# Gated products split tile by tile out of PSUM, a new branch order in the merge, and state-space constants in two parts

## The chip, the cores and the metric

The kernel runs on one core of a Trainium2 chip. Its time is the device time of one execution in microseconds. TensorE multiplies matrices into PSUM, VectorE and ScalarE can read and write PSUM and SBUF, GpSimd works on SBUF alone, and SyncE issues the DMAs that bring weights from HBM. Each engine has its own instruction stream, and they wait for one another through semaphores that are written out by hand in the code.

## What is computed

One decoder layer over two groups of tokens, 256 of a prompt and 64 of a sample, which lie side by side as 320 columns (N). D_MODEL is 2048 and D_FF 5632; everything is float32.

```
x += 0.5 * (silu(h @ w_gate) * (h @ w_up)) @ w_down          # h = RMSNorm(x), first block
z  = RMSNorm(x) @ w_in          # u_ssm, c_q, c_kv, k_r, q_mem, three gates
y_ssm = GLU(gelu(S5(u_ssm)))    # state space: 64 groups of 64 complex modes
y_mla = latent attention(c_q, c_kv, k_r)                     # 16 heads
y_mem = attention to 256 memory tokens(q_mem)                # 4 heads
x += (sig(g_ssm)*(y_ssm@W_ssm) + sig(g_mla)*(y_mla@W_mla) + sig(g_mem)*(y_mem@W_mem)) @ w_out
x += 0.5 * (silu(h @ w_gate) * (h @ w_up)) @ w_down          # second block
y  = RMSNorm(x)
```

## The kernel before

Activations lie feature-major: a tile is 128 features by 320 token columns. A product in float32 is made of three matmuls in the rounded type `fp32r`: operands are split into a high part (rounded) and a low part (the rest), and `three` (lines 396 to 400) adds hi*hi, hi*lo and lo*hi in one PSUM bank.

Weights come in chunks. A full chunk is 256 rows by 512 columns: SyncE loads it into one of three `raw` slots (`load`), ScalarE rounds it to `whi` (line 388), GpSimd subtracts to get `wlo` (line 393), and TensorE multiplies it in `products`: two row tiles q by four column tiles m, three matmuls each, 24 in all. There are four `whi`/`wlo` slots, so weights can be ready up to four chunks ahead. The counter `w_used` tells that TensorE is done with a chunk. The eight PSUM banks make two halves, 0 and 1, of four banks, one bank per column tile; `half_free` tells that a half was read out.

A feed-forward block is a stream of windows of 512 features. The head is `gate` (8 chunks, half 0) and `up` (8 chunks, half 1). Then a loop of ten runs `gate` of the next window, `down` of this one (8 chunks in four windows w of two, on the halves 1, 0, 1, 0) and `up` of the next one. The tail is the last `down`, on the halves 0, 1, 0, 1. VectorE scales the gate by the norm's `rstd` into `silu_g` when the gate is complete, ScalarE applies SiLU, and after the last `up` chunk VectorE multiplies (`prod`, line 1562), rounds (`phi`, line 1573) and subtracts (`plo`, line 1575); `down` needs `phi` and `plo`. In the head and the loop a whole `gate` window stands between these and their `down`; ahead of the tail's `down` nothing does.

The norm's sum of squares is a matmul with ones into bank 7 (`sums`, line 1055), in the head at the seventh `gate` chunk. VectorE makes the mean (line 1372) and its reciprocal (1375), ScalarE the root (734). `up` uses bank 7, so it waits for the mean.

State-space constants (`s5_constants`) are a chain of over a hundred tiny VectorE operations, each waiting for the one before. They stand in VectorE's stream behind the first block's first `silu_g` scaling, ahead of its first products.

The mixer's input projection runs seven windows (`Z_WIN`). In the first, `sums` stands at the sixth chunk. VectorE then runs `powers(0)`, `powers(1)` and `phases(0)` of the state space, and behind them `mean_inv`; then it copies windows 0 and 1 into `u4` (lines 1718, 1719). The first state-space transposes (line 1135) wait for window 1's copy.

The merge loops over four windows of D_MODEL. For each branch: `gate` (8 chunks, half 0) and `branch` (half 1), whose product with the sigmoid gate VectorE adds into `merged`. The order is state space (4 chunks), attention (8 chunks), memory (4 chunks of half size, 12 matmuls each). After the third, `merged` is split into `mhi` (line 1953) and `mlo` (1954) for `out` (8 chunks), which runs after the next window's first gate, or in the tail at once. The merge loop is at line 527, the feed-forward loop at 487.

Of the kernel before, what the change touches and what calls it, by code (L numbers as in the profile page):

```python
# [17 lines left out]
F32 = mybir.dt.float32  # L18
# [56 lines left out]

GR_MEM = (0, 0)
# [41 lines left out]
def build(nc, t_in, t_out):  # L118
    with ExitStack() as ctx:
# [88 lines left out]
        prod = B.take("prod", [4, N])  # L208
# [105 lines left out]
        prod_set = sem("prod_set")  # L314
        prod_hi = sem("prod_hi")
# [86 lines left out]
        def products(e, c, half, n, width, tiles, ahi, alo, k, first, last, cols=N, i=None, per=0):  # L402
# [5 lines left out]
            for q in range(n):  # L408
                for m in range(tiles):
                    a, b = wh[:, q, m * P:(m + 1) * P], wl[:, q, m * P:(m + 1) * P]  # L410
                    ins = three(e, banks[:, 4 * half + m, 0:cols], a, b, ahi[:, k + q, 0:cols], alo[:, k + q, 0:cols],
                                first and q == 0, last and q == n - 1)
            ins.then_inc(w_used, 1)
# [162 lines left out]
        with nc.Block() as block:  # L576

            @block.sync
            def _(e):
# [96 lines left out]
                def merge_load(c, item, i, step, g):  # L676
# [5 lines left out]
                    elif kind == "gate":  # L682
                        c_at = e.snap(i * WIN + (COL_GATE + b * D + WIN)) if step == "body" else COL_GATE + b * D
# [18 lines left out]
            def _(e):  # L702
# [66 lines left out]
                def ffn(name, c0, gr, g):  # L769
                    if name == "ffn2":  # L770
                        next_h(name, g, c0, gr, 1)
# [6 lines left out]
                    def visit(c, kind, k, b, i, per, step):  # L778
                        if c >= c0 + (4 if name == "ffn1" else 3):
# [9 lines left out]
                        if step == "head" and kind == "up" and k == 2:  # L789
                            root(name, rstd)  # L790
# [258 lines left out]
            def _(e):  # L1049
# [34 lines left out]
                def ffn(name, c0, gr):  # L1084
# [3 lines left out]
                    def visit(c, kind, k, b, i, per, step):  # L1088
                        if kind in ("gate", "up"):
                            half = 0 if kind == "gate" else 1  # L1090
                            if step == "head" and kind == "gate":
                                if k == 6:
                                    if name == "ffn2":
                                        e.wait_ge(half_free[1], gr[1])
                                    sums(name, 7)
                                e.wait_ge(hf_lo, AP[name] + k + 1)
                            if step == "head" and kind == "up" and k == 0:
                                e.wait_ge(half_free[1], gr[1])
                                e.wait_ge(mean_ready, 2 * NORM[name] + 1)
                            if k == 0 and step == "body":  # L1100
                                wait(e, half_free[half], gr[half] + (1 if kind == "gate" else 3), i, 3)
                            products(e, c, half, 2, WIN, 4, hhi, hlo, 2 * k, k == 0, k == 7, N, i, per)
                        else:
                            w = k // 2
                            half = (1, 0, 1, 0)[w] if step == "body" else (0, 1, 0, 1)[w]
                            if k < 2:

                                if step == "body":
                                    wait(e, prod_lo, 2 * sbase + k + 1, i, 2)
                                else:  # L1110
                                    e.wait_ge(prod_lo, 2 * (sbase + FFN_BLOCKS - 1) + k + 1)
# [5 lines left out]
                            products(e, c, half, 2, WIN, 4, phi, plo, 2 * (k % 2), k % 2 == 0, k % 2 == 1, N, i, per)  # L1117
# [57 lines left out]
                for w, (c_at, width, half) in enumerate(Z_WIN):  # L1175
                    for k in range(8):
                        for part, s in s5_at.get(8 * w + k, []):
                            s5_pe(part, s)
                        if k == 0:
                            e.wait_ge(half_free[half], seen[half])  # L1180
                            seen[half] += 1
                        if w == 1 and k == 0:
                            e.wait_ge(mean_ready, 2 * NORM["mix"] + 1)
                        if w == 0:
                            if k == 5:
                                e.wait_ge(half_free[1], GR_Z[1])
                                sums("mix", 7)
                            e.wait_ge(hf_lo, AP["mix"] + k + 1)
                        products(e, CH_Z + 8 * w + k, half, 2, width, width // P, hhi, hlo, 2 * k, k == 0, k == 7)
# [869 lines left out]
```

## Time and profile before

| | us |
|---|---|
| median of 3 runs (3240.90 to 3247.93) | 3242.78 |
| the profiled execution's own time | 3241.28 |
| its span, from the first to the last instruction | 3239.5 |
| TensorE's matmuls busy | 3085.8 |
| VectorE busy | 1190.1 |
| ScalarE busy | 1088.1 |
| GpSimd busy | 2037.8 |

The mean granted TensorE clock is 0.975 of full speed. Times in rows are microseconds from the start of the span unless marked ns. PE is TensorE's matmul stream and PEld its weight loads; DVE is VectorE, ACT ScalarE, POOL GpSimd. A line number is that of the kernel before.

### The profile page before, as it was taken

The page shows a single profiled execution, that of the slowest core. Times are in us where ns is not written, and L with a number is a line of the kernel's source. Part 1 is how long each engine was busy: PE and PEld are TensorE (multiplying, and loading weights), DVE is VectorE, ACT ScalarE, POOL GpSimd, SP SyncE. Part 2 cuts the span into 40 slices and gives each one's busy share as a digit, 9 for nine tenths or more (in the row PEclk, how much of TensorE's full clock was granted, in tenths as well). Part 3 has the DMA queues.
Part 4 walks back from the last instruction along what each step waited for, and adds up shares of the span by engine and source line. Part 5 has one row for each costly group of instructions (what it writes and reads, how often), then busy time and mean ns, then how long its engine had stood idle before and what let it go on. Part 6 is the DMA issues. An engine that isn't in the chain of part 4 may idle for free.

```text
span 3239.5 us, 51544 instructions
## 1 busy us (share of the span) xinstructions
PE 3085.8 (95%) x20534; PEld 3050.3 (94%) x20534; DVE 1190.1 (37%) x1944; ACT 1088.1 (34%) x1369; POOL 2037.8 (63%) x876
## 2 busy tenths in 40 slices
PE   7999999999999889699999999998999999999997
PEld 7999999999999889688899999998999999999996
DVE  8832222222226698756623121212522222222223
ACT  5323333333334344323433333332433333333332
POOL 7656666666666344444476766666666666666663
PEclk9999999999999889899999999999999999999998
DMA  6544544444445232223244544444444444444542
GB/s 216 165 124 149 149 149 149 149 149 149 149 149 156 77 103 68 70 70 96 85 150 144 156 142 147 149 146 132 145 150 149 150 148 150 149 149 149 149 149 98
DMA packets 237692, 442.86 MB, mean 137 GB/s; under 512 B 14161, under 2 KB 33169, under 8 KB 237585
## 3 DMA queue, kind: packets, MB, share of 16 engines
q1 hardware_dynamic: 237584, 441.34, 44.9%
q8 instruction: 78, 1.28, 0.2%
q14 instruction: 30, 0.24, 0.0%
HBM read 436.81 MB, written 4.47 MB: 136 GB/s over the span
## 4 chain that ended last, share of the span: by engine, by line
PE 75%; DVE 11%; POOL 7%; issue 6%; ACT 1%; DMA 0%; POOLq 0%; SPq 0%; DVEq 0%; ACTq 0%
PE banks L398 24%; PE banks L399 23%; PE banks L400 23%; POOL wlo L393 7%; DVE hlo L1394 2%; PE banks L1200 1%; DVE hf L1407 1%; DVE elh L1415 1%; DVE s5v L1415 0%; PE banks L1224 0%; DVE mla_p L1745 0%; PE banks L1166 0%; DVE xs L1671 0%; PE banks L453 0%; PE banks L455 0%
## 5 line engine op out<-in xcount | busy, mean ns | idle before, releaser
L393 POOL TENSOR_TENSOR wlo<-raw,whi 128x1024 fp32r<-128x1024 f32 (+4 forms) x848 | 2006.1, 2369 | 1140.1 <-ACT whi L388 1139.8
L388 ACT ACTIVATE whi<-raw 128x1024 fp32r<-128x1024 f32 (+4 forms) x848 | 868.5, 1027 | 1850.3 <-PE banks L400 1728.7
L398 PE MATMUL banks<-hhi,whi 128*128 128x320 f32 (+1 forms) x4016 | 1253.8, 312 | 51.5 <-issue 14.0
L399 PE MATMUL banks<-hlo,whi 128*128 128x320 f32 (+1 forms) x4016 | 1248.3, 311 | 0.0
L400 PE MATMUL banks<-hhi,wlo 128*128 128x320 f32 (+1 forms) x4016 | 1248.2, 311 | 0.0
L398 PEld LDWEIGHTS banks<-hhi,whi 128*128 128x128 f32 x4016 | 763.9, 190 | 54.9 <-issue 33.5
L399 PEld LDWEIGHTS banks<-hlo,whi 128*128 128x128 f32 x4016 | 763.6, 190 | 0.4 <-issue 0.2
L400 PEld LDWEIGHTS banks<-hhi,wlo 128*128 128x128 f32 x4016 | 762.7, 190 | 0.0
L398 PE MATMUL banks<-phi,whi 128*128 128x320 f32 x1408 | 437.8, 311 | 19.9 <-DVE plo L1575 19.9
L399 PE MATMUL banks<-plo,whi 128*128 128x320 f32 x1408 | 437.4, 311 | 0.0
L400 PE MATMUL banks<-phi,wlo 128*128 128x320 f32 x1408 | 437.3, 311 | 0.0
L1533 DVE SCALAR_TENSOR_TENSOR x<-banks,x 128x320 f32<-128x320 f32 x416 | 175.2, 484 | 542.0 <-PE banks L400 542.0
L398 PEld LDWEIGHTS banks<-phi,whi 128*128 128x128 f32 x1408 | 266.5, 189 | 20.7 <-issue 10.5
L399 PEld LDWEIGHTS banks<-plo,whi 128*128 128x128 f32 x1408 | 266.5, 189 | 0.0
L400 PEld LDWEIGHTS banks<-phi,wlo 128*128 128x128 f32 x1408 | 266.4, 189 | 0.0
L1562 DVE TENSOR_TENSOR prod<-banks,silu_g 128x320 f32<-128x320 f32 x88 | 37.0, 483 | 481.3 <-PE banks L400 481.2
L1551 DVE TENSOR_TENSOR silu_g<-banks,rstd 128x320 f32<-128x320 f32 x88 | 37.0, 484 | 388.4 <-PE banks L400 388.4
L1929 DVE TENSOR_TENSOR gate<-banks,rstd_mix 128x320 f32<-128x320 f32 x48 | 20.2, 484 | 254.6 <-PE banks L400 254.6
L398 PE MATMUL banks<-mhi,whi 128*128 128x320 f32 x256 | 80.1, 313 | 9.6 <-DVE mlo L1954 9.6
L1573 DVE CAST phi<-prod 128x640 fp32r<-128x640 f32 x44 | 81.9, 1861 | 0.0
L399 PE MATMUL banks<-mlo,whi 128*128 128x320 f32 x256 | 79.9, 312 | 0.0
L400 PE MATMUL banks<-mhi,wlo 128*128 128x320 f32 x256 | 79.9, 312 | 0.0
(280 smaller groups left out, 2918.3 us busy)
## 6 DMA issues: line engine op xcount, KB each, us to landing
raw<-i_ffn_w_gate SPq DMA_DIRECT2D x176, 512.0 KB, 3.6
raw<-i_ffn_w_up SPq DMA_DIRECT2D x176, 512.0 KB, 3.7
raw<-i_ffn_w_down SPq DMA_DIRECT2D x176, 512.0 KB, 3.6
raw<-i_w_in SPq DMA_DIRECT2D x136, 512.0 KB, 3.7
raw<-i_w_post SPq DMA_DIRECT2D x80, 512.0 KB, 3.6
raw<-i_w_uq SPq DMA_DIRECT2D x16, 384.0 KB, 3.3
raw<-i_w_mem_k SPq DMA_DIRECT2D x8, 512.0 KB, 4.3
raw<-i_w_mem_v SPq DMA_DIRECT2D x8, 512.0 KB, 4.0
```

Source lines behind the costliest of these rows:

```text
L388: e.activation(whi[:, c % SPL, 0:size], raw[:, slot, 0:size], ACT.Copy).then_inc(w_hi, 1)
L393: e.tensor_tensor(wlo[:, c % SPL, 0:size], raw[:, c % RAW, 0:size], whi[:, c % SPL, 0:size].bitcast(F32), ALU.subtract).then_inc(w_lo, 1)
L398: e.matmul(out, hi_s, hi_m, start=start, stop=False)
L399: e.matmul(out, hi_s, lo_m, start=False, stop=False)
L400: return e.matmul(out, lo_s, hi_m, start=False, stop=stop)
L1200: ins = e.matmul(banks[:, bank, col:col + nk], a, b, start=n_ == 0, stop=n_ == len(ops) - 1)
L1394: ins = e.scalar_tensor_tensor(out=hlo[:, t, 0:cols], in0=src[:, t, 0:cols], scalar=gains[:, g + t:g + t + 1], in1=hhi[:, t, 0:cols].bitca ...
L1407: e.tensor_tensor(a, a, square_at(name, p), ALU.add).then_inc(sq_added, 1)
L1533: ins = e.scalar_tensor_tensor(out=x[:, 4 * w + m], in0=banks[:, 4 * half + m, 0:N], scalar=scale, in1=x[:, 4 * w + m], op0=ALU.mult, op1= ...
L1551: ins = e.tensor_tensor(silu_g[:, m], banks[:, m, 0:N], rstd[:], ALU.mult)
L1562: ins = e.tensor_tensor(prod[:, m], banks[:, 4 + m, 0:N], silu_g[:, m], ALU.mult)
L1573: e.tensor_copy(phi[:, t], prod[:, t]).then_inc(prod_hi, 1)
```

## The change

1. In both feed-forward blocks the last `up` chunk runs column tile by column tile, and each of its first three tiles signals `tile_done`. VectorE multiplies each tile in place in PSUM, copies it to `phi` and subtracts to `plo`; `prod` is gone. `down` waits per tile.
2. The same for the third branch of the merge, whose sum with `merged` is also made in PSUM. The branch order becomes state space, memory, attention.
3. In the merge's tail `out` uses the halves 0, 1, 0, 1 and not 1, 0, 1, 0; the second block starts accordingly.
4. `sums` stands ahead of the first `up` chunk (in the mixer, ahead of the second window). That chunk does its first two column tiles for both q first and waits for the mean ahead of the other two.
5. `s5_constants` ends after `V_R4`; the rest is `s5_turns`, run by VectorE behind the first block's first products.
6. In the mixer `powers(1)` and `phases(0)` run behind window 0's copy into `u4`.

```diff
@@ products
+            if by_tile:
+                order = [(q, m) for m in range(tiles) for q in range(n)]
+            elif second_pair:
+                order = [(q, m) for r in range(2) for q in range(n) for m in range(2 * r, 2 * r + 2)]
+            else:
+                order = [(q, m) for q in range(n) for m in range(tiles)]
+            for q, m in order:
+                if second_pair and (q, m) == (0, 2):
+                    second_pair()
+                if operand and m == 0:
+                    operand(q)
...
+                if by_tile and q == n - 1 and m < tiles - 1:
+                    ins.then_inc(tile_done, 1)
@@ merge
-        BR = [("ssm", 4, 2, D), ("mla", 8, 2, D + SSM_W), ("mem", 4, 1, D + SSM_W + HEADS * HD)]
+        BR = [("ssm", 4, 2, D), ("mem", 4, 1, D + SSM_W + HEADS * HD), ("mla", 8, 2, D + SSM_W)]
...
-                        window("out", 0, 2, 2 * w, 1 - w % 2)
+                        window("out", 0, 2, 2 * w, w % 2 if step == "tail" else 1 - w % 2)
@@ tensor, ffn
-                if k == 6:
-                    if name == "ffn2":
-                        e.wait_ge(half_free[1], gr[1])
-                    sums(name, 7)
...
+                                sums(name, 7)
+                                pair = lambda: e.wait_ge(mean_ready, 2 * NORM[name] + 1)
@@ vector, ffn
                             for m in range(4):
...
+                                if m < 3:
+                                    wait(e, tile_done, done + m + 1, i, 3)
                                 else:
+                                    wait(e, w_used, c + 1, i, per)
+                                o = banks[:, 4 + m, 0:N]
+                                e.tensor_tensor(o, o, silu_g[:, m], ALU.mult).then_inc(prod_set, 1)
+                                wait(e, prod_set, 4 * at + m + 1, i, 4)
+                                e.tensor_copy(phi[:, m], o).then_inc(prod_hi, 1)
+                                wait(e, prod_hi, 4 * at + m + 1, i, 4)
+                                ins = e.tensor_tensor(plo[:, m], o, phi[:, m].bitcast(F32), ALU.subtract)
...
+                            if c == CH_FFN1 + 15:
+                                s5_turns()
@@ vector, mixer
                 powers(0)
-                powers(1)
-                phases(0)
                 mean_inv("mix", D, bank=7)
...
+                    if w == 0:
+                        powers(1)
+                        phases(0)
@@ vector, merge, third branch
+                            o = banks[:, 4 + m, 0:N]
+                            e.tensor_tensor(o, o, gate[:, m], ALU.mult).then_inc(merged_set, 1)
+                            wait(e, merged_set, sets + 2 * m + 1, i, 8)
+                            e.tensor_tensor(o, o, merged[:, m], ALU.add).then_inc(merged_set, 1)
+                            wait(e, merged_set, sets + 2 * m + 2, i, 8)
+                            link(e.tensor_copy(mhi[:, m], o))
+                            ins = e.tensor_tensor(mlo[:, m], o, mhi[:, m].bitcast(F32), ALU.subtract)
```

## Rows read from the trace of the kernel before

**Rows 1.** The page: busy share, the chain by engine, and the weight split's group.

```profile
PE 3085.8 (95%) x20534; PEld 3050.3 (94%) x20534; DVE 1190.1 (37%) x1944; ACT 1088.1 (34%) x1369; POOL 2037.8 (63%) x876
...
PE 75%; DVE 11%; POOL 7%; issue 6%; ACT 1%; DMA 0%; POOLq 0%; SPq 0%; DVEq 0%; ACTq 0%
...
L393 POOL TENSOR_TENSOR wlo<-raw,whi 128x1024 fp32r<-128x1024 f32 (+4 forms) x848 | 2006.1, 2369 | 1140.1 <-ACT whi L388 1139.8
```

**Rows 2.** Waits of TensorE: waiter, released by, total us, times, longest us.

```profile
PE banks L398 <- DVE plo L1575: 19.9, 3, 10.2
```

**Rows 3.** Timeline of TensorE: start, us, operation, idle before it in brackets.

```profile
92.50 2.50 PE L1055 MATMUL banks<-hf,ones 128*128 128x320 f32 x4 [2.24 <-DVE hf L1407]
...
168.95 0.63 PE L398 MATMUL banks<-phi,whi 128*128 128x320 f32 x1 [10.25 <-DVE plo L1575]
...
1062.36 0.60 PE L398 MATMUL banks<-hhi,whi 128*128 128x320 f32 x1 [9.64 <-issue]
...
1106.24 0.45 PE L1135 MATMUL banks<-const,bp 128*128 128x128 f32 x1 [5.70 <-DVE u L1719]
...
2248.71 0.61 PE L398 MATMUL banks<-mhi,whi 128*128 128x320 f32 x1 [9.64 <-DVE mlo L1954]
...
3188.28 0.64 PE L398 MATMUL banks<-phi,whi 128*128 128x320 f32 x1 [4.83 <-DVE plo L1575]
```

**Rows 4.** Stretches of TensorE: from:to, length, busy (matmuls touching it), clock, DMA.

```profile
86.57:105.75 19.18, 16.94 (x103) 0.91 0.41 118
151.51:174.91 23.40, 13.15 (x75) 0.78 0.28 91
300.00:400.00 100.00, 100.00 (x684) 1.00 0.51 151
984.50:998.18 13.68, 8.85 (x51) 0.88 0.35 115
1049.04:1068.70 19.66, 10.02 (x50) 0.65 0.15 48
1744.33:1750.24 5.91, 5.58 (x38) 1.00 0.68 180
1906.88:1916.28 9.40, 7.09 (x39) 0.82 0.61 172
2072.92:2080.51 7.59, 5.54 (x39) 1.00 0.71 199
2237.15:2254.18 17.03, 7.39 (x38) 0.70 0.46 155
2275.30:2284.61 9.31, 7.31 (x51) 1.00 0.38 110
```

**Rows 5.** Single lines of VectorE: count, duration ns min/median/max, first and last start.

```profile
L1562 DVE TENSOR_TENSOR prod<-banks,silu_g x88: 479/481/493, 165.9 to 3184.7; 128x320 f32<-128x320 f32 x88
...
L1573 DVE CAST phi<-prod x44: 483/2292/2747, 167.5 to 3188.1; 128x640 fp32r<-128x640 f32 x44
...
L1831 DVE COPY qraw<-banks x8: 479/481/482, 1347.5 to 1533.8; 128x320 f32<-128x320 f32 x8
```

**Rows 6.** Timeline of the mixer's norm on VectorE and ScalarE.

```profile
1061.76 0.49 DVE L1372 TENSOR_SCALAR mean<-banks 128x320 f32<-128x320 f32 x1
1062.29 2.15 DVE L1375 RECIPROCAL mean<-mean 128x320 f32<-128x320 f32 x1
...
1064.48 0.47 ACT L734 ACTIVATE rstd_mix<-mean 128x320 f32<-128x320 f32 x1 [16.04 <-DVE mean L1375]
```

**Rows 7.** The two loops' branches in TensorE's queue: ns min/median/max, first and last start.

```profile
L527 PEldq COMPARE_BRANCH  x3: 79/3695/3961, 1906.9 to 2237.2; - x3
...
L487 PEldq COMPARE_BRANCH  x20: 76/208/240, 225.2 to 3180.8; - x20
```

**Rows 8.** Stretches: length, busy us of PE, PEld, DVE, ACT, POOL (instructions); clock, DMA.

```profile
120.10:164.33 44.23, 38.61 (x264) 38.34 (x262) 41.63 (x74) 12.73 (x12) 28.82 (x13) 1.00 0.48 149
1053.70:1061.75 8.05, 0.00 (x0) 0.00 (x0) 7.70 (x29) 0.00 (x0) 0.00 (x0) 0.57 0.00 0
1064.90:1077.80 12.90, 12.90 (x79) 12.90 (x79) 12.57 (x32) 5.12 (x6) 10.21 (x5) 0.86 0.47 131
```

More of the change, by code:

```diff
@@ L400, in three, with products @@
             return e.matmul(out, lo_s, hi_m, start=False, stop=stop)
-        def products(e, c, half, n, width, tiles, ahi, alo, k, first, last, cols=N, i=None, per=0):
+        def products(e, c, half, n, width, tiles, ahi, alo, k, first, last, cols=N, i=None, per=0, by_tile=False,
+                     second_pair=None, operand=None):
             wait(e, w_lo, c + 1, i, per)
@@ L407, in products @@
             wl = wlo[:, s, 0:n * width].rearrange("p (t c) -> p t c", t=n)
[L408 to L412, printed above, removed]
+            if by_tile:
[9 more added lines that the diff above has]
+                    operand(q)
+                a, b = wh[:, q, m * P:(m + 1) * P], wl[:, q, m * P:(m + 1) * P]
+                ins = three(e, banks[:, 4 * half + m, 0:cols], a, b, ahi[:, k + q, 0:cols], alo[:, k + q, 0:cols],
+                            first and q == 0, last and q == n - 1)
+                if by_tile and q == n - 1 and m < tiles - 1:
+                    ins.then_inc(tile_done, 1)
             ins.then_inc(w_used, 1)
@@ L778, in visit @@
                     def visit(c, kind, k, b, i, per, step):
+                        if step == "head" and kind == "up" and k == 3:
+                            root(name, rstd)
                         if c >= c0 + (4 if name == "ffn1" else 3):
@@ L1116, in visit @@
                                     e.wait_ge(half_free[half], gr[half] + 3 * (FFN_BLOCKS - 1) + 1 + w // 2)
-                            products(e, c, half, 2, WIN, 4, phi, plo, 2 * (k % 2), k % 2 == 0, k % 2 == 1, N, i, per)
+                            products(e, c, half, 2, WIN, 4, phi, plo, 2 * (k % 2), k % 2 == 0, k % 2 == 1, N, i, per,
+                                     operand=operand if k < 2 else None)
                     ffn_stream(e, c0, visit)
@@ L1559, in visit @@
                             wait(e, silu_scaled, base + (2 if body else 1), i, 1)
-                            wait(e, w_used, c + 1, i, per)
+                            done = (TD_FFN1 if name == "ffn1" else TD_FFN2) + (3 if body else 0)
+                            at = base + (1 if body else 0)
                             for m in range(4):
-                                ins = e.tensor_tensor(prod[:, m], banks[:, 4 + m, 0:N], silu_g[:, m], ALU.mult)
-                                if m == 1:
-                                    ins.then_inc(prod_set, 1)
@@ new lines, in merge_dve @@
+                        ins.then_inc(half_free[1], 1)
+                        wait(e, half_free[1], g[1] + before + 1, i, 5)
+                    if kind == "branch" and k == BR[b][1] - 1 and b == 2:
+                        wait(e, gate_ready, (3 if step == "body" else 0) + b + 1, i, 3)
+                        done = TD_MERGE + (3 if step == "body" else 0)
+                        sets = 8 if step == "body" else 0
+                        for m in range(4):
+                            if m < 3:
+                                wait(e, tile_done, done + m + 1, i, 3)
+                            else:
+                                wait(e, w_used, c + 1, i, 48)
+                            o = banks[:, 4 + m, 0:N]
+                            e.tensor_tensor(o, o, gate[:, m], ALU.mult).then_inc(merged_set, 1)
[4 more added lines that the diff above has]
+                            ins = e.tensor_tensor(mlo[:, m], o, mhi[:, m].bitcast(F32), ALU.subtract)
+                            if m < 3:
+                                ins.then_inc(m_split, 1)
+                            else:
+                                ins.then_inc(half_free[1], 1)
+                                wait(e, half_free[1], g[1] + before + 1, i, 5)
```

96 lines of the change are left out of this document (43 added, 53 removed).

## The prediction

> **What bounds the kernel now.** I read the share of busy time first: TensorE is busy 95% of the span and holds 75% of the chain that ended last [rows 1]. So nothing but TensorE's own idle time, and the slow matmuls behind it, can be won. Next I read who TensorE waited for: the named waits are few and long, not many and short. Three waits for `plo` make 19.9 us, the longest 10.2 [rows 2]. The timeline gives their places: 10.25 us ahead of the first `down` window at 168.95, 9.64 us at the second window of the mixer's input projection (1062.36), 5.70 us ahead of the first state-space transposes (1106.24), and 9.64 us ahead of the last `out` windows (2248.71) [rows 3]. The other 19.9 - 10.2 = 9.7 us of `plo` are the end of the two feed-forward streams, 4.83 us each.
>
> Idle time is not the whole price. In a steady stretch 100 us hold 684 matmuls that touch it, some 682 whole ones, so 0.1467 us each and 3.52 us for a chunk of 24 [rows 4]. Stretches that begin and end at the start of a chunk show the true excess. 1049.04 to 1068.70 holds two chunks (7.04 us) and took 19.66: an excess of 12.62, of which 9.64 is idle and 3 is matmuls behind it at the lower of the clock's two levels, since the stretch has a granted clock of 0.65 [rows 4]. I count every stall this way.
>
> **Part 1, gated products tile by tile at the end of the two streams.** Now the split starts after the last matmul: four products, then a cast of 640 columns, then a subtraction, and only then may `down` start. The excess of 984.50 to 998.18 is 13.68 - 7.04 = 6.64 us [rows 4], and the stall at 3188 repeats it. The change lets VectorE start when the first of the four tiles is complete. With tile-major order that is 18 matmuls = 2.64 us before the end E of the chunk. A tile costs three dependent operations of 320 columns. The product out of PSUM takes 0.481 us, a copy out of PSUM 0.481, and I price the subtraction as a product [rows 5]; between dependent ones lie 0.04 us, as between the mean's scaling and its reciprocal [rows 6], so 1.56 us a tile. No row shows VectorE writing into PSUM, which the product now does. Its bounds are 0.4 us, under the shortest product of the trace (479 ns), and 1 us, twice the longest (493) [rows 5]; I take 0.48, since the same operands are read. Tiles are ready at E-1.1, E+0.5, E+2.0, E+3.6. TensorE wants them at E, E+1.76, E+3.52 and E+5.28. No wait is left: 2 x 6.64 = 13.3 us. At 1 us for the write the last tile comes at E+5.7, 0.4 us late; so the end of the range costs little.
>
> The new operations shouldn't stretch while GpSimd runs. Casts from `prod` in SBUF have a median of 2292 ns and a minimum of 483, while products with one operand in PSUM stay within 479 to 493 over 88 of them, though GpSimd splits weights all the time [rows 5]. All three new ones have one operand in PSUM. If the copy alone were blocked for 1.8 us (2292 - 483), the last tile would come at E+5.4, 0.1 late.
>
> One rule speaks against the cut. The Trainium skill (VectorE: DVE Perf Modes, The TRN2 errata) says that each VectorE instruction pays a fixed latency, more for a source in PSUM (120 cycles) than in SBUF (58), so that small tiles pay it often. By its table, as an estimate, the twelve new ones make 12 x 440 cycles = 5.5 us against 4.1 for the four products, two casts and two subtractions of now. The trace's 0.48 us lies near its 440 cycles. But tiles 0 to 2 pay it while TensorE still works on the next tile, so the sum keeps the rows' values and the end of the chain.
>
> **Part 2, the same at the end of the merge**, with the memory branch moved ahead of the attention branch, so the last chunk has 24 matmuls, not 12. The excess of 2237.15 to 2254.18 is 17.03 - 1.76 - 3.52 = 11.75 us [rows 4]. A tile now costs four operations, 2.06 us: ready at E-0.6, E+1.5, E+3.5, E+5.6 against the same four needs, so the fourth is 0.3 to 0.4 us late. Gain 11.3. At 1 us for each of two PSUM writes the fourth comes at E+9.8 and 4.5 us are left.
>
> **Part 3, the new order's other side.** The memory branch's four chunks have half the matmuls, so TensorE eats weights faster than GpSimd refills. Before, the gap after it fell on the loop's top: excess 5.91 - 5.28 = 0.63 where the loop is entered, 9.40 - 5.28 = 4.12 and 7.59 - 5.28 = 2.31 where it turns, 7.06 in all [rows 4]. TensorE's taken branch there took 3.70 and 3.96 us, and 0.24 at most in the feed-forward loop [rows 7]. It started at 1906.9 beside the last twelve matmuls, which end 1.8 us after 1906.88. After a full chunk more work is queued: the last branch of the feed-forward loop started at 3180.8, and its products were done at 3188.28 - 4.83 = 3183.45, a lead of 2.65. So a turn costs 3.96 - 2.65 + 0.2 (to the first matmul, an estimate) = 1.5 and 1.25, and the middle gap of 0.63 now comes four times: 2.5 + 2.75 = 5.3. Gain 1.8, between -2 and +5.
>
> **Part 4, sums moved from the seventh `gate` chunk to ahead of `up`.** At the first norm TensorE waited 2.24 us for the squares and ran four summing matmuls in 2.50 us [rows 3], at half clock, so 1.25 at full. 86.57 to 105.75 took 19.18 for four chunks and the sums: 19.18 - 14.08 - 1.25 = 3.9 us excess [rows 4]. By the time of `up` the squares are long there. The new wait for the mean stands behind twelve matmuls (1.76 us) and needs about 0.55 (a scaling of 320 columns, 0.49 [rows 6]). ScalarE's root waits for mean and reciprocal (2.15 us [rows 6]) and holds up the rounding of weights for about 8 us against three chunks in hand (10.6): nothing. Gain 3.9.
>
> **Part 5, state-space constants in two parts.** This only moves a stall. VectorE's second part took from 120.1 to 164.3, 74 instructions in 44.2 us [rows 8]. Without GpSimd 29 larger ones took 8.05 us, 0.28 each [rows 8]; the small ones I take at 0.25, so 18.3 us of work, and the other 26 are some 12 GpSimd splits of about 2.15 that block it. (A split takes 2.37 [rows 1].) New order: `up` ends at 126.6 (3.9 earlier), products are split at 130.2, and then the second part starts, 10 us later than now. Behind it on VectorE stands the scaling of the next block's `silu_g`, which frees half 0, and TensorE wants that for the second `down` window. `down` starts at 154.8 without a wait, and stops at 161.8. GpSimd stops about 3.5 us later, so to 165.3 ten splits block; 13.6 of 18.3 us are done, the rest runs free to 170.0, and the scaling (four of 0.48) gives 171.9. New stall 10.1 idle plus 2.6 of lower clock, as now, = 12.7, against 23.40 - 10.56 = 12.84 [rows 4]. Gain 0.1. If VectorE stays blocked throughout, the stall is 17 and it costs 7; at best it gains 5.
>
> **Part 6, the mixer.** Now the mean waits behind `powers(0)`, `powers(1)` and `phases(0)`; the last two took 8.05 us [rows 8]. The change puts them behind window 0's copy into `u4`. `powers(0)` ends at 1053.7; the sums end at about 1052.6; the mean is there at 1054.2, when TensorE wants its third tile (1054.4). The root is done near 1056.8 instead of 1064.95 [rows 6], rounding and splitting of the third chunk at 1060.3, 0.6 us late. What comes next: the copy of window 0 takes 12.9 us [rows 8], to 1069.7; then the moved 8 us beside half-size splits, some 12.5; window 1 is complete at 1081.3 and VectorE is ready at 1082.2. The wait at 1106 grows from 5.7 by 0.9. Gain 12.62 - 1.5 = 11.1. If the moved work is blocked as in part 5, it takes 20 and 7 of that is lost.
>
> **Part 7, halves of `out` swapped in the tail.** The next stream's `gate` begins on a half that has been free for 7 us: 9.31 - 7.04 = 2.3 us [rows 4], all gained.
>
> **Sum:** 13.3 + 11.3 + 1.8 + 3.9 + 0.1 + 11.1 + 2.3 = 43.8 us. The profiled execution took 3241.28, 1.5 under the median of 3242.78; minus 43.8 they give 3197.5 and 3199.0. I say 3198.
>
> **Rivals.** (A) This forecast. (B) VectorE swallows part of it: the constants block longer (part 5: 7 more) or the moved state-space work does (part 6: 7 more), as 26 of 44 us blocked [rows 8] speaks for. Against it: GpSimd stops when TensorE does, which caps the stall. Together 3212, one alone 3205. (C) PSUM writes cost 1 us: 43.8 - 5 = 39, 3203; nothing shows them. (D) The new order costs nothing at loop tops and the constants run more freely: 3 to 8 more gained, 3190 to 3195. (E) The change does not do what it says, because the waits that it shortens end on something else at once (weights not split in time): only part 4, 6 and 7 stay, 17 us, 3225. Against it, four chunks lie ready at each of these waits. (F) Slower: the feed-forward loop's branch. It costs 0.2 us, while the merge loop's of nearly twice the matmuls costs 3.7 to 4.0 [rows 7]. The change adds waits to the loop's body and shifts its code. If that pushes it over, each of 18 turns costs 1.5 idle and up to 1.6 of lower clock, 57 us, and the kernel ends 13 us slower at 3256; it decides from 14 of 18 turns. The Trainium skill (Runtime: NRT & Kernel Launch, Instruction fetch mechanics) says that a taken branch whose target isn't in the fetched window waits for a transfer. That agrees with the merge loop's 3.96 us; it makes the place of the code matter and not only its length.
>
> **Chances.** A 0.57, B 0.18, C 0.07, D 0.10, E 0.04, F 0.03, other 0.01. B, C and D end the range: 3187 to 3215. A measurement of this kernel tells about 0.2% (6.5 us) from no change. Faster by more than that: 0.95 (A to E and some of F in one loop alone); within: 0.02; slower: 0.03.
>
> **What the profile after must show.** No TensorE idle time above 0.5 us where `up` turns into the tail's `down` (part 1); under 1 us ahead of the tail's `out` (2); gaps of 1.2 to 1.6 us at two merge loop tops and of 0.3 behind each memory branch (3); none before the first sums (4); about 10 us in front of the second `down` window of the first block, released by `silu_g` and not `plo` (5); under 1 us where 9.64 stood, and 5.7 to 7 ahead of the transposes (6). A VectorE operation that writes PSUM above 0.7 us, a stall of over 12 us in the first block, or a branch of L487 over 1 us would prove the sum wrong.

## The result and the profile after

The changed kernel's median is 3209.91 us (3205.66 to 3215.51), the kernel before beside it 3243.86 (3240.90 to 3247.93); the ratio is 0.9896, with a 95% interval of 0.9876 to 0.9915. It is 34 us faster; 44 were forecast, and 3209.9 lies inside the range of 3187 to 3215. The profiled execution took 3208.56 us, its span 3206.8, with a mean clock of 0.979 against 0.975.

The page of the changed kernel, its busy shares, the chain by engine, and the weight split:

```profile
PE 3079.3 (96%) x20534; PEld 3043.1 (95%) x20534; DVE 1113.2 (35%) x2056; ACT 1087.0 (34%) x1369; POOL 2032.7 (63%) x876
...
PE 71%; DVE 11%; POOL 10%; issue 7%; ACT 1%; DMA 0%; POOLq 0%; SPq 0%; DVEq 0%; ACTq 0%
...
L395 POOL TENSOR_TENSOR wlo<-raw,whi 128x1024 fp32r<-128x1024 f32 (+4 forms) x848 | 2000.7, 2363 | 1112.5 <-ACT whi L390 1112.1
```

TensorE has as many matmuls as in [rows 1], so only idle time and slow matmuls are gone: its idle time fell from 153.7 us (3239.5 - 3085.8) to 127.5, and its busy time by 6.5. Its timeline (columns as in [rows 3]) shows what is left:

```profile
171.17 0.63 PE L400 MATMUL banks<-phi,whi 128*128 128x320 f32 x1 [8.17 <-DVE silu_g L1578]
...
1048.52 0.42 PE L400 MATMUL banks<-hhi,whi 128*128 128x320 f32 x1 [0.58 <-POOL wlo L395]
...
1086.48 0.87 PE L1156 MATMUL banks<-const,bp 128*128 128x128 f32 x3 [9.55 <-DVE u L1747]
...
1896.56 0.41 PE L400 MATMUL banks<-hhi,whi 128*128 128x320 f32 x1 [2.36 <-issue]
...
2061.68 0.41 PE L400 MATMUL banks<-hhi,whi 128*128 128x320 f32 x1 [2.40 <-issue]
...
2225.78 0.31 PE L400 MATMUL banks<-mhi,whi 128*128 128x320 f32 x1
```

All three waits for `plo` or `mlo` at a tail are gone: the last row starts the tail's `out` with no idle time, where [rows 3] had 9.64. The mixer's 9.64 is 0.58. But the wait ahead of the transposes grew from 5.70 to 9.55.

To place every microsecond I number TensorE's chunks from 0 (16 begins the first block, 280 the mixer, 392 the merge, 584 the second block) and compare the same stretch of chunks in both kernels. Stretches of TensorE in the kernel before: from:to, length, busy (matmuls), clock, DMA share, GB/s.

```profile
48.16:105.75 57.59, 55.35 (x318) 0.97 0.53 154
105.75:181.95 76.20, 65.95 (x435) 0.93 0.46 147
181.95:1026.34 844.39, 839.55 (x5715) 1.00 0.50 149
1026.34:1068.70 42.36, 32.45 (x198) 0.84 0.34 100
1068.70:1106.24 37.54, 31.84 (x218) 0.95 0.38 106
1193.36:1286.88 93.52, 85.14 (x594) 0.93 0.29 82
1614.89:2268.26 653.37, 638.34 (x4322) 0.99 0.47 145
2268.26:2302.21 33.95, 31.95 (x219) 1.00 0.45 127
```

The same chunks in the changed kernel:

```profile
49.43:103.00 53.57, 53.57 (x318) 1.00 0.55 158
103.00:176.57 73.57, 65.40 (x435) 0.93 0.47 152
176.57:1014.33 837.76, 837.76 (x5715) 1.00 0.50 150
1014.33:1044.26 29.93, 29.66 (x199) 1.00 0.49 141
1044.26:1086.48 42.22, 32.10 (x218) 0.92 0.35 94
1173.73:1270.12 96.39, 86.79 (x595) 0.91 0.28 80
1599.29:2243.87 644.58, 637.40 (x4323) 1.00 0.48 147
2243.87:2276.07 32.20, 31.91 (x218) 1.00 0.44 120
```

| chunks | part | forecast gain | gain |
|---|---|---|---|
| start to 9 | none | 0 | -1.3 |
| 9 to 25 | 4, sums | 3.9 | 4.0 |
| 25 to 43 | 5, constants | 0.1 | 2.6 |
| 43 to 281 | 1, first tail | 6.6 | 6.6 |
| 281 to 289 | 6, mixer's second window | 12.0 | 12.4 |
| 289 to 300 | 6, wait ahead of the transposes | -0.9 | -4.7 |
| 300 to 393 | none | 0 | -4.2 |
| 393 to 581 | 2 and 3, merge | 13.1 | 8.8 |
| 581 to 590 | 7, halves | 2.3 | 1.7 |
| 590 to the end | 1, second tail | 6.6 | 6.6 |
| sum | | 43.8 | 32.7 |

The first row moves with no change at all: chunk 9 started between 49.2 and 54.0 us in thirteen profiles of kernels with the same code up to there. So a single time says little within 5 us, and the experiments below, of which most ran once, are read by their stretches. "The ninth chunk" and the like in the expectations are these numbers.

### The profile page after: what moved, and what is told of

Read it like the earlier page. It is cut to its first block, busy times and chain, and to the rows that moved or that the text cites. A ratio compares the mean times of both kernels' runs of the same rounds, so it can differ in the third digit from the quotient of the medians.

```text
span 3206.8 us, 51767 instructions
## 1 busy us (share of the span) xinstructions
PE 3079.3 (96%) x20534; PEld 3043.1 (95%) x20534; DVE 1113.2 (35%) x2056; ACT 1087.0 (34%) x1369; POOL 2032.7 (63%) x876
## 4 chain that ended last, share of the span: by engine, by line
PE 71%; DVE 11%; POOL 10%; issue 7%; ACT 1%; DMA 0%; POOLq 0%; SPq 0%; DVEq 0%; ACTq 0%
PE banks L400 22%; PE banks L401 22%; PE banks L402 22%; POOL wlo L395 10%; DVE hlo L1421 1%; PE banks L1221 1%; DVE hf L1434 1%; DVE u L1746 1%; PE banks L1245 0%; DVE mla_p L1776 0%; PE banks L1187 0%; DVE elh L1442 0%; DVE hf L1485 0%; PE banks L469 0%; PE banks L471 0%
## 5 line engine op out<-in xcount | busy, mean ns | idle before, releaser
L1595 DVE TENSOR_TENSOR banks<-banks,silu_g 128x320 f32<-128x320 f32 x88 | 43.3, 492 | 428.9 <-PE banks L402 428.9
L400 PE MATMUL banks<-yahi,whi 128*128 128x320 f32 x256 | 79.1, 309 | 0.0
L401 PE MATMUL banks<-yalo,whi 128*128 128x320 f32 x256 | 79.1, 309 | 0.0
L402 PE MATMUL banks<-yahi,wlo 128*128 128x320 f32 x256 | 79.1, 309 | 0.0
```

The source lines that it names most:

```text
L400: e.matmul(out, hi_s, hi_m, start=start, stop=False)
L401: e.matmul(out, hi_s, lo_m, start=False, stop=False)
L402: return e.matmul(out, lo_s, hi_m, start=False, stop=stop)
L1595: e.tensor_tensor(o, o, silu_g[:, m], ALU.mult).then_inc(prod_set, 1)
```

## The experiments

**The changed kernel again**, beside the next three on the same chip.

> The changed kernel once more, to tell which stretches of its trace repeat and which vary. Theory: what was lost against the forecast is of the order of work, so it repeats: a wait of about 9.5 us ahead of the first state-space transposes, 8 us at the first block's second down window, 2.4 us at the merge loop's two turns. Rival: part of it is chance of this execution: then the first input stage (four waits of 1.2 us on hlo) and the end of the state-space stage (3 us lost where the clock was at its lower level) come out otherwise, with a time 3 to 5 us away from 3208.6.

It took 3210.6 us. Its stretches repeat those of the table within 1.1 us each.

**The mixer's order undone.**

```diff
                 powers(0)
+                powers(1)
+                phases(0)
                 mean_inv("mix", D, bank=7)
...
-                    if w == 0:
-                        powers(1)
-                        phases(0)
```

> The changed kernel, but powers(1) and phases(0) stand ahead of the mean again, as before the change. Theory (the move gives 12 us at the second window and pays 4 us of it back ahead of the transposes): the wait at the second window returns with 8 to 10 us plus slow matmuls (over 10 us in all), the wait ahead of the transposes falls from 9.55 to about 5.7, and the kernel is 6 to 9 us slower than the changed one. Rival (the move is worth nothing since the state-space stage is bound by VectorE anyway): within 3 us of the changed one.

It took 3217.78 us, 7.2 more. But 4.5 of these stood there before the mixer. By stretches (281 to 289, then 289 to 300) it has 39.47 and 38.68 against 29.87 and 42.22 of the kernel above: 9.6 lost, 3.5 won back. TensorE's timeline shows both:

```profile
1055.42 0.63 PE L400 MATMUL banks<-hhi,whi 128*128 128x320 f32 x1 [7.94 <-DVE mean L1399]
...
1097.47 0.87 PE L1156 MATMUL banks<-const,bp 128*128 128x128 f32 x3 [5.71 <-DVE u L1749]
```

So the move is worth 6.1 us up to the transposes. That the totals differ by about as much is luck: the 4.5 us ahead of the mixer are chance, and behind the transposes this run was 3.4 us faster, nearly all of it in stretches that vary from run to run (below).

**The moved work behind window 1's copy instead of window 0's.**

```diff
-                    if w == 0:
-                        powers(1)
-                        phases(0)
+                phases(0)
+                powers(1)
```

> The changed kernel, but phases(0) and powers(1) run behind window 1's copy, not between the two copies. Theory: between the copies they took 16 us beside GpSimd's splits, 4 us more than there was room for, and VectorE idles for 13 us after window 1's copy, so there they cost nothing: wait ahead of the transposes 5.7 us and not 9.55, 4 to 7 us faster than the changed kernel. Rival: they delay the first recurrence instead, and the time stays within 2 us.

It took 3209.7, only 0.9 less; yet it came 2.9 us late out of the first 43 chunks. Its wait ahead of the transposes is back at 5.71, and the stretch 289 to 300 takes 38.37, 3.85 less than 42.22:

```profile
1085.97 1.30 PE L1156 MATMUL banks<-const,bp 128*128 128x128 f32 x5 [5.71 <-DVE u L1747]
```

This settles the cause of the 9.55: the moved work held up window 1's copy, and nothing there needed its results yet. Nor does it hold up what follows: 300 to 393 takes 513.03 here and 513.88 in the kernel above.

**The old branch order.** The split by tiles stays.

```diff
-        BR = [("ssm", 4, 2, D), ("mem", 4, 1, D + SSM_W + HEADS * HD), ("mla", 8, 2, D + SSM_W)]
+        BR = [("ssm", 4, 2, D), ("mla", 8, 2, D + SSM_W), ("mem", 4, 1, D + SSM_W + HEADS * HD)]
```

> The changed kernel with the branch order of before (state space, attention, memory) and all else, the tile-by-tile split too. Theory: the new order does not pay at the loop's turns (branches took 4.8 us and not 3.7 to 4.0 and the gap behind each memory branch comes four times for 0.4), and is worth only the 12 matmuls more of cover in the tail: loop tops and middle gaps together cost 1 to 2 us less than now, the tail waits 1.5 to 2.5 us for mlo, the sum within 2 us of the changed kernel. Rival (my forecast): the old order costs 1.8 us more in the loop and 2 us more in the tail, so about 4 us slower.

It took 3207.88 us. From 393 to 581 it has 645.61; the new order with the same loop has 644.5 to 645.8 in eight of nine profiles (648.3 in one). The order is worth nothing that can be seen, not the 1.8 of part 3: it gives TensorE no wait at the tail, where the old order has one of 0.95 us for `mlo`, and pays for it with three more gaps behind memory branches. The turn of the loop explains why the rest of the forecast gain is missing. TensorE's branch in this kernel (ns min/median/max, first and last start):

```profile
L544 PEldq COMPARE_BRANCH  x3: 79/3856/4275, 1889.8 to 2222.0; - x3
```

The same in the changed kernel:

```profile
L544 PEldq COMPARE_BRANCH  x3: 76/4779/4822, 1891.5 to 2223.4; - x3
```

In the changed kernel the branch starts at 1891.52, the queued matmuls last to 1896.56 - 2.36 = 1894.20, a lead of 2.7 us as forecast; but the branch takes 4.78 and ends 2.1 after them. Before, the lead was 1.9 (1906.88 to 1911.12 - 2.31 = 1908.81), the branch took 3.96 [rows 7] and ended 2.05 after the last matmul. With the old order restored the branch is at 3.86 to 4.28 again. More queued work made the branch longer by as much, and left 2.0 to 2.7 us of idle time in 21 of 22 turns (all profiles with the loop). The odd one is in the run with the constants in one part (below), its branch line being

```profile
L544 PEldq COMPARE_BRANCH  x3: 79/5082/6153, 1895.2 to 2231.0; - x3
```

Here one branch took 6.15 us and TensorE stood idle for 3.89. The next chunk's weights don't explain it, as they were split at 1890.75 (and two further chunks by 1897.80), 10 us before its first matmul at 1901.62. What made this branch longer is open.

**The merge loop written out on TensorE.**

```diff
-            with (loop or (lambda: e.Fori(0, 3)))() as i:
+            if trips:
+                for i in range(trips):
...
-                merge_stream(e, merge_pe)
+                merge_stream(e, merge_pe, trips=3)
```

> TensorE's merge loop is written out three times in its stream, so its two taken branches are gone; all other engines keep the loop. Theory (the turn itself holds TensorE idle 2.1 to 2.6 us whatever is queued ahead of it, and the clock falls behind it): both gaps of 2.3 us vanish, and the merge from its first chunk to the tail's out windows takes 620 to 622.5 us, where the changed kernel took 626.5. Rival of the forecast (part of the wait is work of other engines, refilled weights above all): gaps over 1 us stay at both places, and less than 2 us are gained. A third outcome: the longer code costs gaps of its own in other places.

It took 3202.45 us. Both gaps are gone and each turn of 48 chunks takes 162.55 with 0.39 us of idle time. TensorE, the merge from chunk 393 to 581, and one turn:

```profile
1599.75:2237.80 638.05, 635.27 (x4323) 1.00 0.51 148
1894.61:2057.16 162.55, 162.16 (x1107) 1.00 0.51 149
```

638.05 against 644.58: the two turns cost 6.5 us, 4.8 idle and the rest slow matmuls. The Trainium skill (Runtime: NRT & Kernel Launch, Instruction fetch mechanics) says that a taken branch out of the fetched window waits for a transfer; without the branch there is no such gap here.

**The constants in one part again.**

```diff
                     tt(v[V_R4], v[V_T], v[V_T], ALU.mult)
+                    s5_turns()
...
-                            if c == CH_FFN1 + 15:
-                                s5_turns()
```

> Part 5 alone is undone: the second part of the state-space constants follows at once on the first, ahead of the first block's first products. The forecast had 12.7 us for the new stall against 12.8 for the old: 0.1 us. The traces of the two kernels have 2 to 2.6 us for the stretch that holds it. Theory: 25th to 43rd chunk takes 75.5 to 77 us (73.6 to 74.4 in the changed kernel), with a wait of about 9.5 to 10.5 us in front of the first down window. Rival: the rest of the change already removes the difference (tile by tile products follow the constants at once), and it is within 0.7 us.

It took 3216.1 us. Neither theory had it: the wait is 15.99 us, and 25 to 43 takes 81.37, 7.8 more than with two parts and 5.2 more than before the change. Stretches of TensorE, chunks 9 to 25 and 25 to 43:

```profile
49.53:103.10 53.57, 53.57 (x318) 1.00 0.53 158
103.10:184.47 81.37, 65.38 (x435) 0.90 0.43 138
```

Its timeline has the wait:

```profile
172.05 0.63 PE L400 MATMUL banks<-phi,whi 128*128 128x320 f32 x1 [15.99 <-DVE plo L1600]
```

VectorE's chain of constants takes as long as before: 60.3 us from its first operation to the first product (105.60 to 165.90), and 60.6 in the kernel before (105.24 to 165.88). It sets the time, though TensorE is done with the next window's `gate` 2.6 us sooner (156.06, before 158.70), so those 2.6 us are only waited. The other 3.1 us of the longer wait are a price of part 1: the first `down` window of the loop needs half 1, and the products in place free it only with the last of their twelve operations, 6.15 us after the first began (165.90 to 172.05). Before it was 3.07 (165.88 to 168.95). With the constants in two parts this doesn't show, since nothing waits there.

So parts 1 and 4 without part 5 are worth 57.59 + 76.20 - 53.57 - 81.37 = -1.2 us in these two stretches, and not 3.9. No run has part 4 alone; without the 3.1 it would be some 1.9, an estimate.

**The sums at their old place, with the constants in two parts.** In the first block alone.

```diff
+                                if k == 6 and name == "ffn1":
+                                    sums(name, 7)
                                 e.wait_ge(hf_lo, AP[name] + k + 1)
...
+                                if name == "ffn1":
+                                    e.wait_ge(mean_ready, 2 * NORM[name] + 1)
+                                else:
```

> Part 4 alone is undone in the first block: the sum of squares stands at the seventh gate chunk again, and the first up chunk waits for the whole mean. Theory (with the constants in two parts VectorE's stream hangs on the end of up, so the 4.0 us of the ninth to the 25th chunk come through): 57.5 us there (53.57 in the changed kernel) and the same 73.6 to 74.4 from the 25th to the 43rd, 4 us in all. Rival (VectorE's chain of constants ends at a fixed time whatever up does, as e6_constants_in_one showed for the constants in one part, where 25th to 43rd took 81.4): the 25th to the 43rd chunk takes 70 to 71 us and nothing is lost in all.

It took 3210.56 us. The same two stretches:

```profile
49.51:107.20 57.69, 55.41 (x317) 0.97 0.50 146
107.20:181.04 73.84, 65.65 (x435) 0.93 0.48 152
```

The first stretch loses 4.1, the second keeps 73.8. With the products ahead of the second part, VectorE's chain hangs on `up`, and part 4 comes through in full. Parts 4 and 5 together gave 6.6 us (4.0 and 2.6 in the table); what each is worth depends on whether the other is there.

**Small splits.** GpSimd subtracts only an eighth of the columns in the first block's loop and tail and in three mixer windows. The other low parts of the weights are left out (old values stay there), so this kernel only shows what the splits cost.

```diff
             wait(e, w_hi, c + 1, i, per)
+            if CH_FFN1 + 16 <= c < CH_Z + 24:
+                size = size // 8
```

> In the first block's loop and tail and in the mixer's first three windows GpSimd subtracts only an eighth of each chunk's columns (the rest of the low part keeps old values), so its splits take under 0.5 us and not 2.37. Its output isn't the reference's. Theory (a GpSimd split blocks VectorE's operations on SBUF, one of them per split): no operation of the second part of the constants takes over 1 us, the part takes 18 to 19 us and not 37.9, the wait of 8.19 us at the second down window is gone, and the moved state-space work of the mixer takes 8 to 9 us and not 16.05. Rival (VectorE is slow there for a reason of its own, such as the length of the dependent chain): the part takes over 30 us still and the wait keeps 5 us or more.

It took 3191.63 us, and the wait of 8.2 us for `silu_g` is gone. The constants' second part, then the mixer's moved work, in the changed kernel (length, busy us of PE, PEld, DVE, ACT, POOL with instructions, clock, DMA):

```profile
131.22:169.12 37.90, 31.78 (x217) 31.51 (x215) 35.37 (x73) 9.54 (x9) 21.90 (x10) 0.94 0.45 147
1057.79:1073.84 16.05, 16.05 (x111) 16.05 (x110) 15.75 (x29) 4.55 (x7) 9.95 (x7) 1.00 0.36 95
```

And with small splits:

```profile
132.88:151.50 18.62, 18.62 (x130) 18.62 (x129) 16.08 (x73) 6.13 (x6) 2.48 (x5) 1.00 0.48 157
...
1047.73:1056.20 8.47, 8.47 (x60) 8.47 (x59) 8.00 (x29) 1.27 (x2) 0.72 (x2) 1.00 0.34 91
```

The same 73 and 29 operations take 18.6 and 8.5 us without full splits. VectorE's timeline in the changed kernel shows how:

```profile
132.59 2.36 DVE L1442 TENSOR_TENSOR s5v<-s5v 128x32 f32<-128x32 f32 x1
...
136.10 2.37 DVE L1442 TENSOR_TENSOR uph<-uph 128x32 f32<-128x32 f32 x1
```

And GpSimd's:

```profile
132.49 2.42 POOL L395 TENSOR_TENSOR wlo<-raw,whi 128x1024 fp32r<-128x1024 f32 x1 [1.10 <-ACT whi L390]
136.01 2.42 POOL L395 TENSOR_TENSOR wlo<-raw,whi 128x1024 fp32r<-128x1024 f32 x1 [1.10 <-ACT whi L390]
```

One operation begins 0.1 us after a split does and lasts as long. With small splits (0.47 us) the first of these takes 0.44. The Trainium skill (SBUF — State Buffer, SBUF: two separate sides) says that GpSimd and a VectorE operation with two inputs in SBUF share a pair of ports, which the one that starts first holds for its whole instruction; these rows agree.

**The constants' second part shortened.** Ten operations (two squares of five each) go back to the first part, twelve operations of the doublings to the tail.

```diff
+                def s5_turns():
...
-                    for k in range(3):
+                    double((0, 1), (0, 1))
...
+                        if kind == "down" and k == 0 and step == "tail" and name == "ffn1":
+                            double((2,), (0,))
...
+                            if step == "tail" and w == 0 and name == "ffn1":
+                                double((2,), (1,))
```

> Of the second part of the state-space constants 10 operations (squares, 0.23 us each) go back to the first part, and the last 12 (0.33 us each, the doubling to 128 columns) go to the first block's tail, on either side of window 0's sum. The changed kernel waits 8.19 us at the second down window for the scaling that stands behind this part. Theory (VectorE's stream is what TensorE waits for there, and the tail's VectorE has room): the wait falls by 2.3 + 3.9 us to about 2 us, the stretch from the 25th to the 43rd chunk takes 67.5 to 70 us and not 73.6 to 74.4, and nothing is added in the tail or the mixer: 5 us in all. Rival (the blocked work only shifts: what is moved is blocked by GpSimd elsewhere and the wait keeps 6 to 8 us, or the tail's windows become late by 2 us and more): under 2 us.

It took 3200.8 us. The wait fell to 4.79, and 25 to 43 takes 70.92, so 2.7 us were won there where 5 were expected. The ten operations now lie ahead of the first products, three of them lasting 2.3 us each beside splits, so the first product began at 130.87 and not at 125.27. Another 2.8 us of the low single time are the variation of chunks 319 to 333 (below).

**Twenty-four operations of the doublings in the tail**, 18 ahead of window 0's sum and 6 behind it.

> The last two doublings of the state-space table (24 operations, some 7 us) leave the second part of the constants and stand in the first block's tail, 18 of them ahead of window 0's sum and 6 behind it. e4_turns_shortened moved 12 of them and 10 squares and its wait fell only from 8.19 to 4.79. Theory (what is taken from the part's unblocked end counts in full, what is put between its first part and the products does not): the wait falls by 6.5 to 7 us to 1.2 to 1.7 us, its slow matmuls go too, the stretch from the 25th to the 43rd chunk takes 65 to 67 us (73.6 to 74.4 before), and the tail and the mixer lose at most 1 us of it. Rival (what is moved is blocked there by GpSimd's splits and delays window 0's sum and the mixer's squares): the mixer's first window starts 2 us and more late, and under 5 us are left.

It took 3201.7 us. Theory and rival are both borne out, one at each end, though 5.7 us are left where the rival had under 5. Stretches of TensorE, chunks 25 to 43 and 43 to 281:

```profile
103.83:167.19 63.36, 63.36 (x434) 1.00 0.55 177
167.19:1009.45 842.26, 839.49 (x5715) 1.00 0.50 150
```

The tail's wait in its timeline:

```profile
990.29 0.63 PE L400 MATMUL banks<-phi,whi 128*128 128x320 f32 x1 [2.77 <-DVE x L1563]
```

In the first block the whole stall is gone, 10.2 us. In the tail VectorE's sum comes late, and 842.26 - 837.76 = 4.5 are given back.

**All three together**: these 24 operations, the merge written out, and the moved work behind window 1's copy.

> e8_doubling_in_tail, e5_merge_unrolled and e2_mixer_after_window1 in one kernel. By the stretches of the single runs: 7 from the constants, 6.3 from the merge and 3.8 from the mixer make 17 us against the changed kernel's median of 3209.9, so 3193, and a ratio to the kernel before of 0.984. If the gains don't add (as the sums moved forward and the constants in two parts do not), 3196 to 3200. The time of a single run also moves by up to 5 us with the stretch before the ninth chunk.

The median is 3190.65 us (3187.37 to 3194.02), the ratio to the kernel before 0.9836, interval 0.9820 to 0.9853, against 0.9876 to 0.9915 for the changed kernel: faster than both. Its stretches keep what each had alone: 63.36, 38.39 (289 to 300) and 637.98 (393 to 581). The tail (43 to 281) takes 840.79, so 3.0 us of the first are given back there.

**The doublings spread over three places of the tail.**

```diff
-                            double((1,), (0, 1))
-                            double((2,), (0,))
+                            double((1,), (0, 1))
...
-                            if step == "tail" and w == 0 and name == "ffn1":
-                                double((2,), (1,))
+                            if step == "tail" and w < 2 and name == "ffn1":
+                                double((2,), (w,))
```

> e9_all_three with the moved doublings spread over the tail: 12 operations ahead of window 0's sum, 6 behind it and 6 behind window 1's. In e9 and e8 window 0's sum came 1.2 us too late for the tail's third down window, and 2.77 us idle time and slow matmuls behind it cost 3 to 4.5 us of the 10.2 that the first block had won. Theory (the place alone was wrong): no idle time in the tail, the stretch from the 43rd to the 281st chunk takes 837.8 us again and not 840.8 or 842.3, nothing is lost at the mixer's start, so 3 to 3.5 us less than e9: 3187. Rival (the tail's VectorE has no room: the lateness only goes on to the third window's sum or to the mixer's rounded inputs): under 1 us.

The median is 3191.79 us (3188.79 to 3192.79), the ratio to the kernel before 0.9836 (0.9819 to 0.9854): the rival held. Two stretches, to chunk 281 and from there to 289:

```profile
166.52:1006.44 839.92, 838.02 (x5714) 1.00 0.51 150
1006.44:1041.64 35.20, 32.14 (x199) 0.90 0.42 120
```

The tail is 0.9 better than in the kernel ahead of it (840.79), but the mixer's start loses 5.0 (30.19 there). TensorE's wait of 2.77 us in the tail is gone, but two new ones stand at the mixer's start: 1.90 us for VectorE's sum into `x` (at 1002.82, counted in the first row) and 3.06 for a weight split (at 1016.70). The tail's VectorE has no 7 us to give.

## Why the prediction was right, and where it was not

The places of the gains were right, and 13.2 + 11.5 + 12.4 us of them (parts 1, 2 and 6's second window) came as forecast. The total fell 11 us short in the profiled pair: 4.3 in part 3, 3.8 in the wait ahead of the transposes and 5.5 in the two stretches that no part touches, while part 5 gave 2.5 more than forecast. The time lies in the range because the rivals had widened its upper end. It is partly luck that chance, which moved single times by 5 us and more, didn't carry it over.

**What bounds the kernel.** Right: all 32.7 us of the span came out of TensorE's idle time (26.2) and slow matmuls (6.5).

**Part 1.** Right, 13.2 for 13.3. The unknown cost, VectorE writing into PSUM in place, is 492 ns for the product and 500 for the sum with `merged` (estimate 480), over 88 and 16 operations. None is held up by splits, the longest taking 500 ns:

```profile
L1595 DVE TENSOR_TENSOR banks<-banks,silu_g 128x320 f32<-128x320 f32 x88 | 43.3, 492 | 428.9 <-PE banks L402 428.9
L1597 DVE CAST phi<-banks 128x320 fp32r<-128x320 f32 x88 | 43.3, 492 | 3.0
L1599 DVE TENSOR_TENSOR plo<-banks,phi 128x320 fp32r<-128x320 f32 x88 | 43.2, 491 | 3.0
...
L1985 DVE TENSOR_TENSOR banks<-banks,merged 128x320 f32<-128x320 f32 x16 | 8.0, 500 | 0.5
```

What the forecast weighed and set aside, the longer chain of small operations, is real where TensorE waits for the last tile: 3.1 us in the first block of the run with the constants in one part. At the two tails it starts with the first tile. No run undoes part 1 or 2 alone; their gains are read from the stretches, in which TensorE's wait is gone.

**Part 2.** Right: no idle time ahead of the tail's `out`; of 11.75 us 0.25 is left, so 11.5 for 11.3.

**Part 3.** The step that failed is "a turn costs 3.96 - 2.65 + 0.2". It took the branch's length as fixed and let the longer lead hide it. The branch ends some 2 us after the last queued matmul with either lead; both turns cost 6.5 us, not 2.75. The gaps behind the memory branch measure 0.62 and three times 0.45, 2.0 for 2.5. That makes 7.06 - 8.5 = -1.4 for a forecast of +1.8; the table's 8.8 less part 2's 11.5 is -2.7, and the rest is spread over other chunks. The 7.06 itself was a low draw: with the old order restored the two turns cost 4.0 and 4.4 in excess, where the kernel before had 4.1 and 2.3.

**Parts 4 and 5.** The first is right to 0.1 us in its stretch. Of the second the cause was right (the wait moved to `silu_g` in front of the second `down` window) and its size too large: 8.17 us idle for 10.1, since the second part took 37.9 us (131.22 to 169.12) and not 39.8. (TensorE stopped at 163.0 and not 161.8, but everything there was 1.3 us late from the first row of the table.) The larger fault is in the way the terms stand side by side: 3.9 and 0.1 look like a gain and a move for nothing. Undone one at a time, part 4 is worth 4.1 us in its stretch while part 5 is there, and part 5 7.8 while parts 1 and 4 are; without part 5, parts 1 and 4 together lose 1.2.

**Part 6.** The 12.6 were there (12.4 in the table). The mis-sized term is the moved work: 12.5 us were taken for it, it took 16.05. It takes 8.5 undisturbed, and seven splits, two of them full, lay in it. The wait ahead of the transposes grew by 3.85 where 0.9 was allowed. The forecast had named the bad end (7 us lost) and priced too near the mild one.

**Part 7.** 1.7 for 2.3.

**What no part named.** 4.2 us between chunks 300 and 393, of which 2.9 lie between 319 and 333, where VectorE's state-space recurrence sets the pace. This isn't the change's: the changed kernel's mixer code gave 93.5, 93.5, 93.6, 95.3, 96.4, 96.4, 97.1 and 99.2 us there in eight profiles. In the changed kernel splits and the scaling of `ckvT` lengthen three operations in a row, where one of the profiles with 93.5 us (the constants in one part) has two:

```profile
1250.19 2.97 DVE L1706 TENSOR_TENSOR_SCAN v_im<-dec,xs 128x324 f32<-128x324 f32 x1
1253.21 3.02 DVE L1709 TENSOR_TENSOR xs<-v_re,ee 128x324 f32<-128x324 f32 x1
...
1256.16 2.67 DVE L1710 TENSOR_TENSOR s_t<-v_im,ee 128x324 f32<-128x324 f32 x1
```

What decides on which operations they fall is open; so is why the memory's first chunks take up to 5 us longer in some executions.

**The rivals.** B, at 0.18, came nearest in its mechanism: VectorE swallowed 3.8 us of part 6, though none of part 5. C is refuted by 492 ns. D came half: the constants gave 2.5 us more than forecast, but the loop tops cost more and not nothing. F didn't come: both feed-forward loops run without a gap over 0.1 us in TensorE. E is refuted by both tails.

## What to carry to other kernels

A stall that one engine's fixed chain causes isn't shortened by bringing the other engine to it sooner; move work out of the chain first, and price such edits together. Cutting a product into tiles pays where the consumer can start with the first tile, and lengthens the chain where it needs the last one. Small operations on SBUF wait for what GpSimd does beside them, here for as long again as they take themselves, so put them where nothing waits behind them, and keep one operand in PSUM where something does. Compare two executions stretch by stretch: totals that differ by 7 us held 4.5 us of chance.

## What the hardware showed beyond that

A taken branch of the long merge loop on TensorE took 3.7 to 5.1 us in 21 of 22 turns, ending 1.8 to 2.4 us after the matmuls queued ahead of it (the other one 6.15 and 3.6), while the feed-forward loop's took 0.2 [rows 7]; with the merge loop written out nothing of it was left, and the longer code cost no gap of its own. A VectorE operation of 0.19 us lasts 2.36 when a split of GpSimd began just before it, while operations of 320 columns with one operand in PSUM stay at 489 to 500 ns beside the same splits.
